# Key projections of the neighbourhood attention: two result banks of their own in place of the ring of six

## What is computed

```
for l in range(2):
    mod = silu(c) @ w_ada[l] + b_ada[l]              # shifts, scales, gates
    h = rms_norm(x) * (1 + sc1) + sh1
    x = x + g1 * mixer(h)
    h = rms_norm(x) * (1 + sc2) + sh2
    x = x + g2 * grouped_moe(h)                      # 32 experts, top 2 of one group
mixer(h):
    qg, kg, vg, gg, lf, lb, qn, kn, vn = split(h @ w_in)
    o_gla = gated linear attention of qg, kg, vg in both directions, decays from lf, lb
    o_na  = neighbourhood attention of rms_norm(qn), rms_norm(kn), vn on the 8 x 64 grid
    return concat(o_gla * silu(gg), o_na) @ w_out
```

## Time and profile before

| | us |
|---|---|
| median of 3 runs | 1976.39 |
| lowest and highest of them | 1972.84, 1978.12 |
| the profiled execution's own time | 1976.45 |
| its span in the trace | 1974.7 |
| PE busy | 1617.4 (82% of the span) |
| DVE busy | 935.2 (47%) |
| level stage of layer 0, from kn0 to the last transposes | about 171 to 268 |
| the same stage of layer 1 | about 1135 to 1232 |

### The profile page before, as it was taken

The page is one execution under the profiler, slowest core; times in us unless marked ns, Lnnn a source line. Parts: engine busy times, 40 slices in busy tenths (PEclk is TensorE's granted clock), DMA queues, the critical chain, the costliest instruction groups (busy, mean ns, idle before and its releaser), DMA issues.

```text
span 1974.7 us, 29955 instructions
## 1 busy us (share of the span) xinstructions
PE 1617.4 (82%) x9962; PEld 972.8 (49%) x9962; DVE 935.2 (47%) x1825; ACT 324.1 (16%) x690; POOL 291.9 (15%) x402
## 2 busy tenths in 40 slices
PE   3998897955997878997849988978399789998874
PEld 1474445853554445554426634467355455554441
DVE  3866757144443333443367476643533344343334
ACT  1242236020000000000032323341000000000000
POOL 0003221001211111121100141300101111111110
PEclk9999998977999999999979999989599999999997
DMA  8951252642999999899488214424369999999995
GB/s 258 312 162 44 85 150 86 256 171 96 381 396 412 405 409 406 358 407 408 191 276 273 75 42 146 154 118 185 131 267 408 408 407 391 412 402 408 410 398 205
DMA packets 150930, 538.59 MB, mean 273 GB/s; under 512 B 16942, under 2 KB 109342, under 8 KB 117566
## 3 DMA queue, kind: packets, MB, share of 16 engines
q1 hardware_dynamic: 135440, 514.17, 67.8%
q0 software_dynamic: 11520, 16.82, 2.6%
q10 hardware_dynamic: 3888, 6.61, 1.0%
HBM read 533.34 MB, written 25.20 MB: 283 GB/s over the span
## 4 chain that ended last, share of the span: by engine, by line
PE 47%; DMA 31%; DVE 8%; issue 6%; SPq 5%; ACT 2%; DVEq 0%; POOL 0%; POOLq 0%; ACTq 0%
PE bank L564 43%; DMA ring<-w 17%; DMA pool_b<-w 7%; DMA pool_a<-xn_rows,tok_now 2%; DMA y_rows<-pool_a,row_now 2%; PE bank L856 2%; DMA pool_b<-b_ada 2%; SPq L430 1%; DVE low L1254 1%; PE bank L878 1%; DVE ring L1433 1%; SPq L415 1%; ACT pool_a L1136 1%; DMA pool_a<-y_rows 1%; SPq L414 1%
## 5 line engine op out<-in xcount | busy, mean ns | idle before, releaser
L564 PE MATMUL bank<-ring,pool_a 128*64 128x256 f32 (+2 forms) x3968 | 557.7, 445 | 112.2 <-DMA ring<-w 67.4
L564 PEld LDWEIGHTS bank<-ring,pool_a 128*64 128x64 f32 (+1 forms) x3968 | 294.7, 143 | 353.3 <-issue 193.8
L564 PE MATMUL bank<-hT,ring 128*128 128x512 f32 (+1 forms) x672 | 304.3, 609 | 32.9 <-DVE pool_b L1418 29.3
L1693 DVE TENSOR_SCALAR pool_a<-pool_a 128x256 f32<-128x256 f32 x72 | 21.4, 297 | 590.2 <-ACT pool_a L1165 590.2
L564 PEld LDWEIGHTS bank<-hT,ring 128*128 128x128 f32 (+1 forms) x672 | 126.9, 192 | 194.2 <-issue 158.2
L1165 ACT ACTIVATE pool_a<-bank 128x256 f32<-128x256 f32 x72 | 27.6, 383 | 1041.5 <-PE bank L564 1041.5
L564 PE MATMUL bank<-ring,hT 128*128 128x256 f32 x768 | 168.6, 380 | 1.9 <-ACT hT L1150 1.9
L564 PEld LDWEIGHTS bank<-ring,hT 128*128 128x128 f32 x768 | 144.9, 190 | 25.7 <-issue 6.4
L1694 DVE RECIPROCAL pool_a<-pool_a 128x256 f32<-128x256 f32 x72 | 126.2, 1753 | 2.5
L1706 DVE TENSOR_TENSOR pool_a<-bank,g_bc 64x512 f32<-64x512 f32 x144 | 99.2, 689 | 40.6 <-PE bank L564 36.4
L564 PE MATMUL bank<-hT,pool_a 128*64 128x256 f32 x768 | 92.8, 396 | 22.0 <-DMA hT<-w 22.0
(11 more groups left out here) (272 smaller groups left out, 1564.1 us busy)
## 6 DMA issues: line engine op xcount, KB each, us to landing
ring<-w SPq DMA_DIRECT2D x129, 2048.0 KB, 26.1
pool_b<-w SPq DMA_DIRECT2D x22, 2048.0 KB, 25.6
hT<-w SPq DMA_DIRECT2D x22, 2048.0 KB, 21.1
low<-w SPq DMA_DIRECT2D x22, 2048.0 KB, 23.0
ring<-w_ada SPq DMA_DIRECT2D x40, 1024.0 KB, 12.1
ring<-w_in SPq DMA_DIRECT2D x24, 1024.0 KB, 5.8
pool_b<-w_ada SPq DMA_DIRECT2D x16, 1024.0 KB
ring<-w_out SPq DMA_DIRECT2D x8, 1024.0 KB, 10.5
```

The source lines that it names most:

```text
L564: return nc.tensor.matmul(out, lhsT, rhs, start=start, stop=stop, skip_group_check=True)
L1693: own(V.tensor_scalar(e1, e1, 1.0, None, ALU.add), t, 2)
```

## The change

The four key tiles leave the ring. ("kn", 0) and ("kn", 2) go into bank 6, ("kn", 1) and ("kn", 3) into bank 7, where only kn2 and kn3 wait, for kn0 and kn1. The other 177 tiles of a layer are numbered anew, without the four, and go into six banks by that number; each waits for the tile six places before it in the shortened list.

```diff
+    side = {("kn", i): 6 + i % 2 for i in range(4)}
+    in_ring = [key for key, _ in plan if key not in side]
+    place = {key: n for n, key in enumerate(in_ring)}
...
+        def bank_of(key):
+            return bank[side[key] if key in side else place[key] % RING]
+
+        def held_before(key):
+
+            if key in side:
+                return (key[0], key[1] - 2) if key[1] >= 2 else None
+            return in_ring[place[key] - RING] if place[key] >= RING else None
...
         def free_bank(pe, l, key):

-            n = index[key]
-            if n >= RING:
-                who, count = taken[plan[n - RING][0]]
+            held = held_before(key)
+            if held is not None:
+                who, count = taken[held]
                 took = act_took if who == "a" else dve_took
                 pe.wait_ge(took.s, took.at(l, count))
-            return bank[n % RING]
+            return bank_of(key)
```

More of the change, by code:

```diff
@@ L344, in build @@
         route_exp = sig("route_exp", 1)
+        def bank_of(key):
[4 more added lines that the diff above has]
+            return in_ring[place[key] - RING] if place[key] >= RING else None
         def ready(eng, l, key):
             eng.wait_ge(tile_ready.s, tile_ready.at(l, index[key] + 1))
-            return bank[index[key] % RING]
+            return bank_of(key)
         passed = {id(e): sig(n, 0) for e, n in ((nc.sync, "passed_sp"), (nc.tensor, "passed_pe"),
```

## The result

The changed kernel takes 1940.43 us (median of 6 runs, 1938.18 to 1944.67) against 1977.57 us of the kernel before (6 runs, 1972.84 to 1981.39). The ratio on record is 0.9819, with a 95% interval of 0.9806 to 0.9832; the two medians alone give 0.9812, which lies inside it. The forecast was 1941.6, its range 1935 to 1952. The profiled execution took 1940.22 us, with a span of 1938.4.

A forecast was written before the change was run, and what follows sets the result against it. PE's waits for DVE's key tiles and the slow clock behind them were taken to bound the level stage, with DVE last after the change. Gains of 17.5 and 17.3 us, 34.8 off 1976.45, gave 1941.6 us; range 1935 to 1952.

The forecast's parts named there:

- Four waits of PE for a key tile: In the level stage PE waits four times, 14.6 us in all, for DVE to take a key tile.
- The clock term: Slow PE clock over kn1 and vf0 behind pauses above 5 us: 4.43 us in layer 0, 4.16 in layer 1.
- PE's schedule: Level stage, layer 0, PE alone: kn1 at 181.40, rounds of 10.37 us, ada4 at 231.37, 19.06 us ahead.
- three places at which DVE gates PE: Bank waits in the level stage, including vf1 and level 5's first pair: close, but no wait of PE.
- DVE's schedule: Layer 0: DVE runs 8.6 us ahead from the sum of pieces 16 and 17, ends its next sum at 232.75.
- Beside POOL DVE is slower: Rival, chance 0.11: multiplications behind level 1 run 1.51 us longer, ada4 4.5 us later in each layer; 1948 to 1960.
- ada4 waits for DVE's sum, 1.5 us: Before ada4 PE needs the sum of pieces 18 and 19: 232.9, not 231.4, DVE last by 1.5 us.
- Pieces 18 and 19: Transfers for DVE's sum before ada4: landing taken as 11.35 us behind the first issue, at 225.0, before 226.2.
- the rival with 20.5 us: Rival, chance 0.05: loads for DVE's sum land 20.5 us behind issue, 7.9 us too late in each layer; 1957.4.
- 17.5 and 17.3 us a layer: Time by which ada4 comes earlier in layer 0 and layer 1; total 34.8 us.
- All that follows moves along: Behind ada4, query tiles, first experts' weights and attention are released by PE tiles and move with it; query tiles 17 us earlier.
- Double-buffering brings nothing: Rule against the change: double-buffering PSUM gave another kernel's unbroken projections no further gain; time would stay at 1976.

The follow-up runs named there:

- the filled pauses: Five idle matmuls on PE ahead of kn1 and of vf0, added to the kernel before with its waits kept; 1971.92 us, 0.9980 of the kernel before.
- the load on DVE: Six more multiplications on DVE ahead of level 5's copies: added to the kernel before, 1977.27 us; added to the changed kernel, 1955.78 us.

## Why the prediction was right, step by step

- *Four waits of PE for a key tile set the stage.* Right, and shown from both sides: the waits vanish when the keys have two banks, and three of them return to the hundredth when they have one.
- *The clock term, 4.43 and 4.16 us.* Right; the filled pauses gave 4.39 and 4.16 back in the level stages with the waits in place. That it fits to some hundredths is in part luck, since the slow tiles vary: in the profile of the kernel before with the load on DVE they cost 4.37 and 4.59 us. The Trainium skill (TensorE: Matmul & The Clock Gate, What's actually happening) says that the default clock is the throttled one and that activity releases it; the kernel with busy work in the pause agrees, 7.13 us a tile at 1.00.
- *PE's schedule.* With the 1.57 us by which the stage began later, kn1 was forecast at 182.97, kn2 at 193.34, kn3 at 203.71, vf1 at 223.13. They stood at 182.90, 193.20, 203.51 and 223.13. That vf1 fits to the hundredth is luck. A round took 10.30 us and not 10.37, so PE was 0.27 us ahead of the schedule at level 5 (220.87 against 221.14), and lost these 0.27 at a wait that the prediction didn't have. It names three places at which DVE gates PE, lists two of them and finds no wait; the third is level 5's second pair, which needs DVE's third copy of level 4.
- *DVE's schedule.* The sum of 16 and 17 was forecast at 206.67 and began at 206.53; the sum of 18 and 19 at 227.77, and began at 227.65. Between the two lie two errors that cancel, which is luck. I had kept the 8.6 us of the first sum and 4.0 us for line 1409 and the subtractions behind it. The sum took 10.0 us (206.53 to 216.56), and the multiplication with its subtractions 2.5 (to 219.02). POOL's two subtractions, in the kernel before beside DVE's, now ran beside the sum. DVE and POOL before, then POOL after:

```profile
223.54 1.41 DVE L1367 TENSOR_TENSOR ring<-ring 128x512 f32<-128x512 f32 x1
224.88 1.52 DVE L1368 TENSOR_TENSOR ring<-ring 128x512 f32<-128x512 f32 x1
...
222.87 1.54 POOL L1779 TENSOR_TENSOR ring<-ring 128x512 f32<-128x512 f32 x1 [6.43 <-PE bank L564]
224.37 1.48 POOL L1780 TENSOR_TENSOR ring<-ring 128x512 f32<-128x512 f32 x1
...
214.00 1.18 POOL L1792 TENSOR_TENSOR ring<-ring 128x512 f32<-128x512 f32 x1 [4.75 <-PE bank L577]
215.14 1.22 POOL L1793 TENSOR_TENSOR ring<-ring 128x512 f32<-128x512 f32 x1
```

- *Beside POOL DVE is slower* was the rival at 0.11. Its premise came true: line 1422 took 3.29 us at 196.73, against 1.23 at the same place before. Its consequence did not, since both subtractions behind it took 0.69, and the group 4.6 us as before. The conflict moved from one instruction to its neighbour and didn't grow: before, DVE's multiplication began 0.46 us ahead of POOL's and the first subtraction behind it took 2.72 us; after, it began 0.14 us behind POOL's, and took the longer time itself. The Trainium skill (SBUF — State Buffer, Who interferes with whom) says that a DVE instruction with two inputs from the main buffer contends with a POOL instruction that reads it; the trace agrees, with 3.29 us for the multiplication at 196.73, beside POOL's of 196.59, and 1.21 for the one at 216.56, beside no work of POOL.
- *ada4 waits for DVE's sum, 1.5 us.* It waited 1.24, and that DVE ends last there is shown by the load: nothing before, 13.4 us after.
- *Pieces 18 and 19.* DVE took them without a wait 12.0 us behind the first issue at 215.69 (the row `215.69 0.54 SPq L427 DMA_DIRECT2D ring<-w_ada  x1`), so they had landed by then and the rival with 20.5 us is out. When exactly they landed the trace doesn't show.
- *17.5 and 17.3 us a layer.* It was 17.75 and 17.47. The sum of 34.8 measured 35.2; the other 1.1 us between the two profiles is no merit of the forecast.
- *All that follows moves along.* From ada4 to the next stage's first matmul it took 50.30 us before and 50.29 after, in layer 0. The expert stages differ by 3 us between two profiles of the changed kernel alone.
- *Double-buffering brings nothing*, which the prediction took from the Trainium skill's finding on another kernel (TensorE: Matmul & The Clock Gate, HAM oscillation), didn't hold here; the 35 us are measured. Here a key tile held its bank across the next level's work, kn1 from 186.91 to the end of its key tile at 200.34. That this is what makes the difference to that kernel is not shown.

## What to carry to other kernels

In a ring of result tiles that are handed on in order, look for the tile that is read last long after it was written; it stops whatever comes one turn later, and the wait is printed on that innocent tile. Give such tiles banks of their own, as many as the number of them alive at once: one bank left half of the gain. Then walk the next engine's schedule before adding up the waits, since the removed idle time was also its cover, and price pauses of some microseconds on PE with the slow tile behind them.

## What was not expected of the hardware

The short pauses showed a finer picture of PE's clock than the kernel before did. Pauses of 1.03, 1.50, 1.53 and 1.61 us left the next tile at 7.13 us, and that of 1.24 us left ada4 at 0.64 and vf2 behind it at 7.13; one of 2.09 us (2.10 in layer 1) was followed by 8.78 us (8.68) at a granted clock of 0.81, as much as behind some pauses of 5.5 us (8.71). How long a tile is slow is not set by the length of the pause alone: 5.5 us gave 8.71 and 9.66 before, 8.81 with all keys in one bank, and 9.80 and 9.94 with the load on DVE in the kernel before; 5.98 us gave 9.98 and 8.76, 8.83 and 8.91 with that load, and 9.15 and 9.10 with only the first key out of the ring. And a float32 matmul call of 512 columns stands as two rows and takes 0.87 us (11 calls from 183.54 to the next tile at 193.09).
